# Loading the input and the first two weight blocks in four feature parts, with both projections run part by part

## The chip, the cores and the metric

The kernel runs on one core of a Trainium2 chip. The metric is the device time of one execution in microseconds, the median of several. Before the change it is 2222.32 us (three runs, 2222.03 to 2223.93).

## What is computed

The reference is a stack of three blocks on one sequence of 512 tokens with 1024 features, all in 32-bit floats. Only the very beginning matters here:

```
h = rms_norm(x, norm_g[layer])      # x: 512 x 1024
p = h @ w_in[layer]
c_q, c_kv, k_r, gate_a, dil_qkv, gate_b = split(p)
```

`dil_qkv` holds queries, keys and values of three groups of dilated attention; the queries and keys are rotated by tables of sine and cosine. After two layers of this come a feed-forward block, a mix of a recurrence and windowed attention, and a second feed-forward block.

## The kernel before

It is written by hand, engine by engine, with a semaphore for each kind of event; every engine executes its instructions strictly in the order of its own program.

**Layout.** The input is kept transposed: X holds eight tiles (k = 0 to 7) of 128 features by 512 tokens. The input rows are loaded into XIN (part of ARENA) by SyncE and turned by TensorE in 32 transposes of 128x128 (lines 1082 to 1091), eight for each pair of tiles, which VectorE copies from PSUM to X (line 2038).

**Three-part products.** Each operand of a large product is split in a high part (ScalarE, rounded to fp32r) and a low part (VectorE, the rest). A product is then three matmuls, high by high, low by high and high by low (`three`, lines 870 to 872). For X they are UH (`hi_of_gained`, line 1309, which also applies the gain of the norm) and UL (`lo_of_gained`, line 1767). For the weights they are WH (`hi_of_chunk`, line 1290) and WL (`lo_of_chunk`, line 1716).

**Weight chunks.** Weights come in chunks of 1024 rows by 256 columns (1 MB), numbered in order of use: chunk 0 is the first query projection q0, chunk 1 the key projection k0, chunk 2 the value projection v0, chunk 3 q1, chunk 4 k1. WS, WH and WL each have two slots, for even and odd chunks. SyncE loads chunk c into WS when chunk c-2 has been split completely (`load`, line 773, semaphore w_split). ScalarE makes the high part of chunk c when the product with chunk c-2 is finished. A `feature_major` product (q and k) is eight steps k of six matmuls of 512 columns, a `token_major` one (v) 96 matmuls of 256 columns.

**The norm.** The inverse root mean square of each token is applied after the products. ScalarE squares the tiles of X (line 1299), VectorE adds them up in RB (lines 1729 and 1732), TensorE sums over partitions (`norm_sum`, line 920) and, after VectorE has taken the reciprocal, turns it back (`norm_spread`, line 936); ScalarE copies it to RI (line 1322). With RI, VectorE scales the rotation tables (lines 2096 and 2097) and then rotates q0 and k0 (`rotated`, lines 1806 to 1817).

**The order at the start.** TensorE: one small transpose of the gains, 32 transposes of the input, q0, the transposes of all gain vectors and one small product for a bias table (lines 1124 and 1128), k0 with the norm's parts between its steps, v0, q1, k1. VectorE takes the results of lines 1124 and 1128 in `vectors` and `bias_rows` (lines 2043 to 2056), and computes eight small values in `softplus` (lines 2063 to 2077), between which it waits for an exponential from ScalarE (line 1523). GpSimd's queue loads the rotation tables (line 814) and the masks (line 815), ScalarE's queue the small vectors.

## Time and profile before

| what | value |
|---|---|
| median of three runs | 2222.32 us |
| lowest and highest run | 2222.03 and 2223.93 us |
| the profiled execution's own time | 2223.23 us |
| its span | 2221.4 us |
| TensorE busy (matmul) | 96% of the span |
| VectorE, ScalarE, GpSimd busy | 52%, 35%, 2% |
| DMA, mean over the span | 85 GB/s |

The span is the time from the first to the last recorded instruction of the profiled execution; its own time is 1.8 us longer. TensorE is busy nearly all the time, so what counts is where it waits, and at which clock it runs. The chain of work that ended last lies on TensorE for 87% of the span, on VectorE for 8%. All that the change touches lies in the first 80 us.

### The profile page before, as it was taken

What the parts mean: (1) busy time and instruction counts of PE and PEld (TensorE: products, weight loads), DVE (VectorE), ACT (ScalarE), POOL (GpSimd) and SP (SyncE); (2) the same over time, 40 slices, a digit from 0 to 9 for tenths busy, and PEclk for the clock granted to TensorE, in tenths of its full rate; (3) what the DMA queues carried; (4) which work ended last, traced back from release to release, by engine and by line L of the source; (5) the groups of instructions that cost most, each with busy time, mean ns of one, the idle gap of its engine ahead of it and who ended that gap; (6) DMA issues with size and microseconds to landing.
All of it is one profiled execution on the core that took longest, in us unless ns stands there. A gap on an engine that the chain in (4) does not pass through costs nothing.

```text
span 2221.4 us, 28281 instructions
## 1 busy us (share of the span) xinstructions
PE 2130.4 (96%) x11693; PEld 1756.8 (79%) x11693; DVE 1160.5 (52%) x1593; ACT 775.7 (35%) x1229; POOL 40.0 (2%) x75
## 2 busy tenths in 40 slices
PE   6999999999999999989999998999999989999997
PEld 5888878678888887767888887787688877888886
DVE  5655557645565556746333335775653446333334
ACT  3251434633241535524222224353632234222223
POOL 0101000000001000000000000000000000000000
PEclk9999999999999999999999999999999999999998
DMA  5423222013313122123233321234023221333221
GB/s 161 114 58 95 77 76 77 22 58 109 100 39 114 58 69 67 39 86 114 94 95 103 103 98 57 76 114 133 21 87 102 96 94 58 95 95 108 99 95 38
DMA packets 157280, 188.49 MB, mean 85 GB/s; under 512 B 4018, under 2 KB 147700, under 8 KB 157044
## 3 DMA queue, kind: packets, MB, share of 16 engines
q1 hardware_dynamic: 152256, 174.34, 24.9%
q0 software_dynamic: 4464, 12.47, 1.8%
q8 instruction: 79, 1.29, 0.2%
q14 instruction: 29, 0.24, 0.0%
q10 hardware_dynamic: 452, 0.15, 0.0%
HBM read 181.68 MB, written 7.36 MB: 85 GB/s over the span
## 4 chain that ended last, share of the span: by engine, by line
PE 87%; DVE 8%; ACT 3%; issue 2%; DMA 1%; SPq 0%; DVEq 0%; ACTq 0%
PE PS L870 26%; PE PS L872 25%; PE PS L871 25%; PE PS L956 4%; PE PS L997 2%; PE PS L968 2%; DVE WL L1716 1%; PE PS L1075 1%; DVE TMP L1966 1%; DVE UL L1767 1%; ACT PR L1362 1%; DMA ARENA<-in_x 1%; ACT PR L1359 0%; DVE PS L1822 0%; DVE X L1974 0%
## 5 line engine op out<-in xcount | busy, mean ns | idle before, releaser
L870 PE MATMUL PS<-UH,WH 128*128 128x512 f32 x1712 | 677.1, 396 | 28.5 <-DVE UL L1767 17.5
L872 PE MATMUL PS<-UH,WL 128*128 128x512 f32 x1712 | 670.5, 392 | 0.0
L871 PE MATMUL PS<-UL,WH 128*128 128x512 f32 x1712 | 670.1, 391 | 0.0
L1290 ACT ACTIVATE WH<-WS 128x2048 fp32r<-128x2048 f32 x103 | 197.3, 1916 | 630.0 <-PE PS L872 630.0
L870 PEld LDWEIGHTS PS<-UH,WH 128*128 128x128 f32 x1712 | 324.2, 189 | 102.5 <-issue 26.5
L872 PEld LDWEIGHTS PS<-UH,WL 128*128 128x128 f32 x1712 | 323.6, 189 | 68.7
L871 PEld LDWEIGHTS PS<-UL,WH 128*128 128x128 f32 x1712 | 324.3, 189 | 66.9 <-issue 0.7
L1716 DVE TENSOR_TENSOR WL<-WS,WH 128x2048 fp32r<-128x2048 f32 x103 | 235.8, 2289 | 238.2 <-ACT WH L1290 238.0
L1987 DVE TENSOR_TENSOR WL<-WS,WH 128x2048 fp32r<-128x2048 f32 x44 | 100.7, 2289 | 157.9 <-ACT WH L1445 157.9
L1445 ACT ACTIVATE WH<-WS 128x2048 fp32r<-128x2048 f32 x44 | 84.3, 1917 | 264.5 <-PE PS L872 264.5
L870 PE MATMUL PS<-HH,WH 128*128 128x512 f32 x352 | 136.9, 389 | 0.0
L871 PE MATMUL PS<-HL,WH 128*128 128x512 f32 x352 | 136.9, 389 | 0.0
L872 PE MATMUL PS<-HH,WL 128*128 128x512 f32 x352 | 136.9, 389 | 0.0
L870 PE MATMUL PS<-WH,UH 128*128 128x256 f32 x416 | 118.5, 285 | 0.0
L871 PE MATMUL PS<-WL,UH 128*128 128x256 f32 x416 | 117.7, 283 | 0.0
L872 PE MATMUL PS<-WH,UL 128*128 128x256 f32 x416 | 117.7, 283 | 0.0
L968 PE MATMUL PS<-IDN,PR 128*128 128x128 f32 x624 | 89.3, 280 | 17.6 <-DVE PT L1851 7.5
L968 PEld LDWEIGHTS PS<-IDN,PR 128*128 128x128 f32 x624 | 66.4, 140 | 42.7 <-issue 28.9
L997 PE MATMUL PS<-PT,ARENA 128*64 128x128 f32 x1248 | 84.7, 279 | 1.3 <-DVE ARENA L1876 1.3
L2004 DVE TENSOR_TENSOR ARENA<-PS,RI 128x1024 f32 (+1 forms) x22 | 26.9, 1224 | 112.3 <-PE PS L872 112.3
L870 PEld LDWEIGHTS PS<-WH,UH 128*128 128x128 f32 x416 | 79.7, 192 | 1.0 <-issue 0.2
L871 PEld LDWEIGHTS PS<-WL,UH 128*128 128x128 f32 x416 | 79.7, 192 | 0.6 <-issue 0.2
(270 smaller groups left out, 2713.2 us busy)
## 6 DMA issues: line engine op xcount, KB each, us to landing
WS<-in_ffn_w SPq DMA_DIRECT2D x66, 1024.0 KB, 5.2
WS<-in_w_in SPq DMA_DIRECT2D x64, 1024.0 KB, 5.4
WS<-in_w_out SPq DMA_DIRECT2D x8, 1024.0 KB, 5.2
WS<-in_w_gate SPq DMA_DIRECT2D x8, 1024.0 KB, 5.4
WS<-in_w_attn_out SPq DMA_DIRECT2D x4, 1024.0 KB, 5.1
WS<-in_w_lru_out SPq DMA_DIRECT2D x4, 1024.0 KB, 5.2
WS<-in_w_o SPq DMA_DIRECT2D x4, 1024.0 KB, 5.1
bias_skewed<-bias_rows POOLq DMA_DIRECT2D x1, 3072.0 KB, 14.7
```

Of the source, the lines that this page charges most:

```text
L870: nc.tensor.matmul(dst, sh, mh, start=start, stop=False, skip_group_check=True)
L871: nc.tensor.matmul(dst, sh, ml, start=False, stop=False, skip_group_check=True)
L872: return nc.tensor.matmul(dst, sl, mh, start=False, stop=stop, skip_group_check=True)
L956: last[b] = nc.tensor.matmul(acc[:, c0:c0 + w], q, k, start=start, stop=True, skip_group_check=True)
L968: last = nc.tensor.transpose(bank(4 + b)[:, k * P:(k + 1) * P], PR[:, n % 2, b * S + k * P:b * S + (k + 1) * P], IDN[:, :])
L997: last = nc.tensor.matmul(dst, v, PT[:, n % 2, k * P:(k + 1) * P], start=start, stop=stop, skip_group_check=True)
L1075: last = nc.tensor.matmul(pair(key)[:, w, :], RGW[:, w, 2 * j + m, :], XC[:, m, :], start=True, stop=True)
L1290: nc.scalar.activation(WH[:, c % 2, 0:kt * n], WS[:, c % 2, 0:kt * n], ACT.Copy).then_inc(w_hi, 1)
L1445: nc.scalar.activation(WH[:, c % 2, :], WS[:, c % 2, :], ACT.Copy).then_inc(w_hi, 1)
L1716: tt(WL[:, c % 2, 0:kt * n], WS[:, c % 2, 0:kt * n], WH[:, c % 2, 0:kt * n].bitcast(F32), ALU.subtract).then_inc(w_split, 1)
L1987: tt(WL[:, c % 2, :], WS[:, c % 2, :], WH[:, c % 2, :].bitcast(F32), ALU.subtract).then_inc(w_split, 1)
L2004: tt(hid, pair((f, "w3", 0)), ri, ALU.mult).then_inc(dve_out, 1)
```

## The change

The input is loaded in four parts of 256 features (all tokens), each followed by the same 256 rows of chunk 0 and of chunk 1; each part has its own semaphores. Rotation tables and masks are issued only when the last input part has landed. TensorE turns one input part, multiplies what it can of q0 and k0, turns the next, and so on (`input_turned`, `first_step`); ScalarE and VectorE split input and weights by the same parts. q0 and k0 are thus worked on together, the norm's two TensorE parts move into v0, the small transposes and the bias product move between the steps of k0, and their results are taken by VectorE before it copies the last input part. The high and low parts of chunks 2 and 3 are both made before VectorE takes the reciprocal of the norm. The PSUM banks change where that is needed.

```diff
--- before.py
+++ after.py
@@ -489,7 +489,10 @@
-        x_in = sem("x_in")
+        x_in = [sem(f"x_in{f}") for f in range(4)]
+        first_in = [sem(f"first_in{f}") for f in range(4)]
+        first_hi = sem("first_hi")
+        first_lo = sem("first_lo")
...
@@ -606,6 +609,13 @@
+        def landing(c):
+
+            return 16 * (c // 2)
+
+        def first_part(t, c, f):
+            return slot(t, c, KD, CW)[:, 2 * f:2 * f + 2, :]
+
@@ -763,13 +773,17 @@
-            for r in range(NT):
-                sp.dma_start(XIN[:, r, :], a["x"][0].rearrange("(i r) d -> r i d", r=NT)[r]).then_inc(x_in, 16)
+            for f in range(4):
+                feats = slice(f * CW, (f + 1) * CW)
+                sp.dma_start(XIN[:, :, feats], a["x"][0][:, feats].rearrange("(i r) d -> i r d", r=NT)
+                             ).then_inc(x_in[f], 16)
+                for c in range(2):
+                    sp.dma_start(slot(WS, c, KD, CW)[:, 2 * f:2 * f + 2, :],
+                                 chunk_source(pl.chunks[c][0])[:, 2 * f:2 * f + 2, :]).then_inc(first_in[f], 16)
 
             def load(c, src):
                 key, kt, n, _ = pl.chunks[c]
-                if c >= 2:
-                    sp.wait_ge(w_split, c - 1)
+                sp.wait_ge(w_split, c - 1)
                 sp.dma_start(slot(WS, c, kt, n), src).then_inc(landed[c % 2], 16)
...
-            c = 0
+            c = 2
@@ -811,6 +825,7 @@
             pool.dma_start(SK[:, :], bass.AP(a["attn_sinks_2"].tensor, 0, [[0, P], [1, QH]])).then_inc(rel_in, 16)
+            pool.wait_ge(x_in[3], 16)
             pool.dma_start(TAB, a["rotation"]).then_inc(tabs_in, 16)
             pool.dma_start(MASK[:, :, :], a["dil_mask"]).then_inc(tabs_in, 16)
             pool.wait_ge(small_dve, 3)
@@ -897,13 +912,17 @@
-            def token_major(key):
+            def token_major(key, norm=None):
 
                 c = pl.chunk[key]
                 take_pair(key)
                 weights(c)
                 acc = pair(key).rearrange("p a (b n) -> p (a b) n", b=2)
                 for k in range(KD):
+                    if norm and k == 2:
+                        norm_sum(norm, KD)
+                    if norm and k == 4:
+                        norm_spread(norm)
                     for t in range(NT):
                         tok = slice(t * P, (t + 1) * P)
 
@@ -1078,17 +1097,71 @@
 
             pe.wait_ge(identity_in, 16)
             pe.wait_ge(gains_in, 16)
-            nc.tensor.transpose(bank(5)[:, 0:FIRST], ROWS[0:FIRST, 0, :], IDN[0:FIRST, 0:FIRST]).then_inc(small_pe, 1)
-            pe.wait_ge(x_in, 16 * NT)
-            for j in range(4):
-                key = ("xt", j)
-                take_pair(key)
+            nc.tensor.transpose(bank(7)[:, 0:FIRST], ROWS[0:FIRST, 0, :], IDN[0:FIRST, 0:FIRST]).then_inc(small_pe, 1)
+
+            def input_turned(f):
+
+                key = ("xt", f)
+                pe.wait_ge(x_in[f], 16)
+                if f == 1:
+                    pe.wait_ge(small_dve, 1)
+                if f >= 2:
+                    pe.wait_ge(dve_out, pl.dve_out["xt", f - 2])
                 for m in range(2):
                     for r in range(NT):
                         last = nc.tensor.transpose(pair(key)[:, m, r * P:(r + 1) * P],
-                                                   XIN[:, r, (2 * j + m) * P:(2 * j + m + 1) * P], IDN[:, :])
+                                                   XIN[:, r, (2 * f + m) * P:(2 * f + m + 1) * P], IDN[:, :])
                 last.then_inc(acc_ready, 1)
+
+            def first_step(c, k):
+
+                key = pl.chunks[c][0]
+                pe.wait_ge(lo_done, pl.lo[("x", 0), k])
+                if k < 6:
+                    pe.wait_ge(first_lo, k // 2 * 2 + c + 1)
+                else:
+                    weights(c)
+                for m in range(2):
+                    part = slice(m * P, (m + 1) * P)
+                    last = three(pair(key)[:, m, :], slot(WH, c, KD, CW)[:, k, part], slot(WL, c, KD, CW)[:, k, part],
+                                 UH[:, k, :], UL[:, k, :], k == 0, k == KD - 1)
+                if k == KD - 1:
+                    last.then_inc(acc_ready, 1)
+
+            def vectors_turned():
+                pe.wait_ge(dve_out, pl.dve_out["xt", 2])
+                pe.wait_ge(consts_in, 16 * vector_dmas)
+                for i in range(2):
+                    n = min(P, NVEC - i * P)
+                    last = nc.tensor.transpose(bank(5)[:, i * P:i * P + n], ROWS[0:n, i, :], IDN[0:n, 0:n])
+                last.then_inc(small_pe, 1)
+
+                pe.wait_ge(rel_in, 48)
+                nc.tensor.matmul(bank(4)[0:QH, 0:384], TBL, ONEHOT, start=True, stop=True).then_inc(small_pe, 1)
+
+            input_turned(0)
+            first_step(0, 0)
+            input_turned(1)
+            first_step(0, 1)
+            first_step(0, 2)
+            input_turned(2)
+            first_step(0, 3)
+            first_step(1, 0)
+            first_step(1, 1)
+            first_step(0, 4)
+            input_turned(3)
+            first_step(0, 5)
+            first_step(1, 2)
+            first_step(1, 3)
+            vectors_turned()
+            first_step(1, 4)
+            first_step(1, 5)
+            first_step(0, 6)
+            first_step(0, 7)
+            first_step(1, 6)
+            first_step(1, 7)
             pe.wait_ge(const_ok, 2)
+
...
@@ -1106,27 +1179,19 @@
             for L in range(DEPTH):
                 for hh in range(2):
                     for i, (w, g) in enumerate(DILATED_ORDER):
+                        if L == 0 and hh == 0 and i < 2:
+                            continue
                         if w == "v":
                             if hh == 0 and g == 0:
                                 if L == 0:
                                     pe.wait_ge(small_dve, 3)
+                                    pe.wait_ge(dve_out, pl.dve_out["xt", 3])
                                 else:
                                     results_taken(pl.item_at["mla", L - 1][1])
-                            token_major((w, L, hh, g))
+                            token_major((w, L, hh, g), ("x", 0) if (L, hh, g) == (0, 0, 0) else None)
                         else:
                             feature_major((w, L, hh, g), new=("x", L) if hh == 0 and i == 0 else None,
                                           norm=("x", L) if hh == 0 and i == 1 else None)
-                        if L == 0 and hh == 0 and i == 0:
-
-                            pe.wait_ge(consts_in, 16 * vector_dmas)
-                            for i in range(2):
-                                n = min(P, NVEC - i * P)
-                                last = nc.tensor.transpose(bank(5 + i)[:, 0:n], ROWS[0:n, i, :], IDN[0:n, 0:n])
-                            last.then_inc(small_pe, 1)
-
-                            pe.wait_ge(rel_in, 48)
-                            nc.tensor.matmul(bank(7)[0:QH, 0:384], TBL, ONEHOT, start=True, stop=True
-                                             ).then_inc(small_pe, 1)
                     pe.wait_ge(rope_done, pl.rope["k", L, hh, 2])
                     attention(("dil", L, hh), lambda: token_major(("v", L, hh, 2)))
                 for j in range(2):
@@ -1496,15 +1560,21 @@
             for L in range(DEPTH):
                 if L == 0:
                     act.wait_ge(small_dve, 1)
-                    for k in range(KD):
-                        hi_of_gained(("x", L), k, (dve_out, pl.dve_out["xt", k // 2]))
-                        if k == 3:
-                            hi_of_chunk(0)
-                    hi_of_chunk(1)
+                    for f in range(4):
+                        for k in (2 * f, 2 * f + 1):
+                            hi_of_gained(("x", L), k, (dve_out, pl.dve_out["xt", f]))
+                        act.wait_ge(first_in[f], 32)
+                        for c in range(2):
+                            nc.scalar.activation(first_part(WH, c, f), first_part(WS, c, f), ACT.Copy
+                                                 ).then_inc(first_hi if f < 3 else w_hi, 1)
+                        squares(("x", L), lambda k: X[:, k, :], (2 * f, 2 * f + 1))
+                else:
+                    squares(("x", L), lambda k: X[:, k, :], range(KD))
+                table(ACT.Sqrt)
                 c0 = pl.chunk["q", L, 0, 0]
-                squares(("x", L), lambda k: X[:, k, :], range(KD))
-                table(ACT.Sqrt)
                 hi_of_chunk(c0 + 2)
+                if L == 0:
+                    hi_of_chunk(c0 + 3)
                 rms(("x", L), D)
                 copy_inverse(("x", L))
 
@@ -1516,7 +1586,7 @@
-                        if hh == 1 or i > 0:
+                        if hh == 1 or i > (L == 0):
                             hi_of_chunk(pl.chunk[key] + 2)
                         if L == 0 and hh == 0 and i == 2:
                             act.wait_ge(small_dve, 4)
@@ -2031,17 +2101,13 @@
             dve.wait_ge(small_pe, 1)
-            nc.vector.tensor_copy(G[:, 0:FIRST], bank(5)[:, 0:FIRST]).then_inc(small_dve, 1)
-            for j in range(4):
-                key = ("xt", j)
-                ready(key)
-                nc.vector.tensor_copy(X[:, 2 * j:2 * j + 2, :], pair(key)).then_inc(dve_out, 1)
+            nc.vector.tensor_copy(G[:, 0:FIRST], bank(7)[:, 0:FIRST]).then_inc(small_dve, 1)
 
...
@@ -2079,17 +2145,31 @@
                 if L == 0:
-                    for k in range(KD):
-                        lo_of_gained(("x", L), k)
-                        if k == 3:
-                            lo_of_chunk(0)
-                    lo_of_chunk(1)
-                add_squares(("x", L), 0, KD)
+                    for f in range(4):
+                        key = ("xt", f)
+                        ready(key)
+                        nc.vector.tensor_copy(X[:, 2 * f:2 * f + 2, :], pair(key)).then_inc(dve_out, 1)
+                        for k in (2 * f, 2 * f + 1):
+                            lo_of_gained(("x", L), k)
+                        for c in range(2):
+                            if f < 3:
+                                dve.wait_ge(first_hi, 2 * f + c + 1)
+                            else:
+                                dve.wait_ge(w_hi, c + 1)
+                            tt(first_part(WL, c, f), first_part(WS, c, f), first_part(WH, c, f).bitcast(F32),
+                               ALU.subtract).then_inc(first_lo if f < 3 else w_split, 1)
+                        add_squares(("x", L), 2 * f, 2 * f + 2)
+                        if f == 2:
+                            vectors()
+                            bias_rows()
+                else:
+                    add_squares(("x", L), 0, KD)
                 if L == 0:
-                    vectors()
-                    bias_rows()
+                    lo_of_chunk(c0 + 2)
+                    lo_of_chunk(c0 + 3)
                 inverse(("x", L))
-                lo_of_chunk(c0 + 2)
+                if L:
+                    lo_of_chunk(c0 + 2)
                 if L == 0:
                     dve.wait_ge(tabs_in, 32)
                 dve.wait_ge(inv_copied, pl.copied["x", L])
@@ -2100,7 +2180,7 @@
                         key = (w, L, hh, g)
                         if w != "v":
                             rotated(key)
-                        if hh == 1 or i > 0:
+                        if hh == 1 or i > (L == 0):
                             lo_of_chunk(pl.chunk[key] + 2)
                         if L == 0 and hh == 0 and i == 1:
                             softplus()
```

The order of instructions on VectorE, from the start. Before (L2038 copies to X, L1767 makes UL, L1716 makes WL, L1732 adds squares, L2043 takes the vectors):

```order
L2038 COPY X<-PS 128x1024 [waits acc_ready] x4
L1767 SCALAR_TENSOR_TENSOR UL<-X,G,UH 128x512 [waits hi_done] x4
L1716 TENSOR_TENSOR WL<-WS,WH 128x2048 [waits w_hi]
L1767 SCALAR_TENSOR_TENSOR UL<-X,G,UH 128x512 [waits hi_done] x4
L1716 TENSOR_TENSOR WL<-WS,WH 128x2048 [waits w_hi]
L1729 COPY RB<-SQ 128x512 [waits sq_ready]
L1732 TENSOR_TENSOR RB<-RB,SQ 128x512 [waits sq_added,sq_ready] x7
L2043 COPY G<-PS 128x112 [waits small_pe]
```

In the change, its third and fourth part (L2151 copies to X, L1837 makes UL, L2159 makes WL, L1802 adds squares, L2109 takes the vectors, L2119 the bias table; L1786 are the low parts of chunks 2 and 3):

```order
L2151 COPY X<-PS 128x1024 [waits acc_ready]
L1837 SCALAR_TENSOR_TENSOR UL<-X,G,UH 128x512 [waits hi_done] x2
L2159 TENSOR_TENSOR WL<-WS,WH 128x512 [waits first_hi] x2
L1802 TENSOR_TENSOR RB<-RB,SQ 128x512 [waits sq_added,sq_ready] x2
L2109 COPY G<-PS 128x112 [waits small_pe]
L2110 COPY G<-PS 128x34
...
L2119 TENSOR_SCALAR PT<-PS 16x384 [waits small_pe]
L2122 TENSOR_SCALAR NSK<-SK 128x16 [waits rel_in]
L2151 COPY X<-PS 128x1024 [waits acc_ready,dve_step]
L1837 SCALAR_TENSOR_TENSOR UL<-X,G,UH 128x512 [waits hi_done] x2
L2159 TENSOR_TENSOR WL<-WS,WH 128x512 [waits w_hi] x2
L1802 TENSOR_TENSOR RB<-RB,SQ 128x512 [waits sq_added,sq_ready] x2
L1786 TENSOR_TENSOR WL<-WS,WH 128x2048 [waits w_hi] x2
L1808 RECIPROCAL RC<-RC 128x4 [waits std_ready]
```

The four copies to X, which stood together, now stand apart, and the wait for the vectors' transposes (small_pe) stands ahead of the fourth; the low parts of chunks 2 and 3 now both stand ahead of the reciprocal.

The order on TensorE around the vectors' transposes. Before, between the last step of q0 and the first of k0:

```order
L872 MATMUL PS<-UH,WL 128x512
L1124 MATMUL PS<-IDN,PR 128x128 [waits consts_in]
L1124 MATMUL PS<-IDN,PR 128x34
L1128 MATMUL PS<-PT 16x384 [waits rel_in]
L870 MATMUL PS<-UH,WH 128x512 [waits w_split,dve_out]
```

In the change, between steps 3 and 4 of k0:

```order
L887 MATMUL PS<-UH,WL 128x512
L1136 MATMUL PS<-IDN,PR 128x128 [waits consts_in,dve_out]
L1136 MATMUL PS<-IDN,PR 128x34
L1140 MATMUL PS<-PT 16x384 [waits rel_in]
L885 MATMUL PS<-UH,WH 128x512 [waits first_lo,lo_done]
```

They stood behind 48 matmuls of q0. Now they stand behind ten steps (steps 0 to 5 of q0, 0 to 3 of k0, 60 matmuls) and all 32 transposes of the input, and ahead of the last six steps.

## Rows read from the trace of the kernel before

**Rows 1.** The page's first part: busy time, share of the span, instructions.
```profile
PE 2130.4 (96%) x11693; PEld 1756.8 (79%) x11693; DVE 1160.5 (52%) x1593; ACT 775.7 (35%) x1229; POOL 40.0 (2%) x75
```
**Rows 2.** Busy time by stage; the last three columns are granted clock, DMA share, GB/s.
```profile
0.00:13.30 13.30, 0.26 (x1) 0.18 (x1) 0.17 (x1) 0.00 (x0) 3.23 (x11) 1.00 0.87 289
13.30:16.60 3.30, 3.27 (x16) 3.04 (x16) 1.22 (x1) 0.00 (x0) 0.00 (x0) 1.00 1.10 348
...
19.00:22.90 3.90, 0.00 (x1) 0.00 (x0) 3.86 (x6) 3.90 (x6) 0.00 (x0) 1.00 0.03 11
22.90:25.30 2.40, 0.00 (x0) 0.00 (x0) 2.40 (x3) 2.40 (x5) 0.00 (x0) 0.50 0.00 0
25.30:29.70 4.40, 4.33 (x10) 3.47 (x11) 4.40 (x5) 2.31 (x3) 0.00 (x0) 0.50 0.79 235
...
51.90:63.60 11.70, 11.70 (x97) 11.47 (x95) 11.47 (x14) 1.92 (x1) 0.00 (x0) 1.00 0.28 89
63.60:64.90 1.30, 0.00 (x1) 0.00 (x0) 1.30 (x2) 1.26 (x4) 0.00 (x0) 1.00 0.00 0
```
**Rows 3.** TensorE in order of time: start, duration, engine, line, [idle before <-releaser].
```profile
13.32 3.04 PEld L1088 LDWEIGHTS PS<-IDN,ARENA 128*128 128x128 f32 x16 [7.56 <-DMA ARENA<-in_x]
16.61 0.85 PEld L1088 LDWEIGHTS PS<-IDN,ARENA 128*128 128x128 f32 x8 [0.25 <-DVE X L2038]
...
25.37 0.77 PE L870 MATMUL PS<-UH,WH 128*128 128x512 f32 x1 [6.37 <-DVE WL L1716]
...
38.39 0.45 PE L1124 MATMUL PS<-IDN,PR 128*128 128x128 f32 x2
...
39.51 0.50 PE L870 MATMUL PS<-UH,WH 128*128 128x512 f32 x1
...
50.10 0.60 PE L936 MATMUL PS<-IDN,RB 128*128 128x128 f32 x4
...
64.97 0.47 PE L870 MATMUL PS<-UH,WH 128*128 128x512 f32 x1 [1.37 <-DVE WL L1716]
75.98 0.39 PE L870 MATMUL PS<-UH,WH 128*128 128x512 f32 x1
```
**Rows 4.** VectorE in order of time.
```profile
15.33 4.94 DVE L2038 COPY X<-PS 128x1024 f32<-128x1024 f32 x4 [9.25 <-PE PS L1088]
20.18 2.73 DVE L1767 SCALAR_TENSOR_TENSOR UL<-X,G,UH 128x512 fp32r<-128x512 f32 x4
22.83 2.28 DVE L1716 TENSOR_TENSOR WL<-WS,WH 128x2048 fp32r<-128x2048 f32 x1
...
38.88 0.28 DVE L2043 COPY G<-PS 128x112 f32<-128x112 f32 x1 [2.99 <-PE PS L1124]
...
40.09 0.15 DVE L2056 TENSOR_SCALAR NSK<-SK 128x16 f32<-128x16 f32 x1
...
51.43 0.69 DVE L2096 TENSOR_TENSOR ARENA<-ARENA,RI 128x512 f32<-128x512 f32 x1 [0.82 <-ACT RI L1322]
...
62.54 2.29 DVE L1716 TENSOR_TENSOR WL<-WS,WH 128x2048 fp32r<-128x2048 f32 x1
...
68.57 0.17 DVE L2067 TENSOR_SCALAR SP__84<-SP__84 128x8 f32<-128x8 f32 x1 [3.67 <-ACT SP__84 L1523]
...
72.04 2.29 DVE L1716 TENSOR_TENSOR WL<-WS,WH 128x2048 fp32r<-128x2048 f32 x1
```
**Rows 5.** ScalarE in order of time.
```profile
16.66 1.28 ACT L1309 ACT_TABLE_LOAD   x1 [16.66 <-DVE X L2038]
17.95 2.56 ACT L1309 ACTIVATE UH<-X,G 128x512 fp32r<-128x512 f32 x4
...
50.73 0.60 ACT L1322 ACTIVATE RI<-PS 128x512 f32<-128x512 f32 x1 [3.06 <-PE PS L936]
```
**Rows 6.** Groups by line and shape: busy, mean ns of one, idle before.
```profile
L1290 ACT ACTIVATE WH<-WS 128x2048 fp32r<-128x2048 f32 x103 | 197.3, 1916 | 630.0 <-PE PS L872 630.0
L1380 ACT ACTIVATE WH<-WS 128x512 fp32r<-128x512 f32 x36 | 22.8, 633 | 0.0
L1930 DVE TENSOR_TENSOR WL<-WS,WH 128x512 fp32r<-128x512 f32 x36 | 24.7, 686 | 14.5 <-ACT WH L1380 14.5
```
**Rows 7.** DMA: landing of the four input loads (L767); weight loads up to 60 us.
```profile
DMA to landing us min/median/max: 4.2/6.3/11.1
WS<-in_w_in SPq DMA_DIRECT2D x5, 1024.0 KB, 5.5
```

More of the change, by code:

```diff
@@ L1376, in hi_part @@
                 if i == 0:
-                    act.wait_ge(landed[c % 2], 16 * (c // 2 + 1))
+                    act.wait_ge(landed[c % 2], landing(c))
                     act.wait_ge(acc_ready, pl.acc[pl.chunks[c - 2][3]])
@@ L1442, in hi_in_loop @@
                     c = c0 + b
-                    act.wait_ge(landed[c % 2], 16 * i + 16 * ((c + 2) // 2 + 1))
+                    act.wait_ge(landed[c % 2], 16 * i + landing(c + 2))
                     act.wait_ge(acc_ready, 2 * i + (pl.acc[f, "w1", 0] + b))
```

11 lines of the change are left out of this document (5 added, 6 removed).

## Prediction

> **What bounds the kernel now.** I read the page's shares first. TensorE is busy for 2130.4 us of a span of 2221.4 [rows 1], so a change can take from the 91 us in which it stands still, or from its slow clock. The change touches only the start, so the second view is the stages of the first 65 us. TensorE does nearly nothing in the first 13.3 us, while the DMA engines are busy for 87% of the time at 289 GB/s [rows 2]. Then it turns the input, stands still from 19.0 to 25.3 and runs ten matmuls at a granted clock of 0.50 (the 1.2 GHz level), the rest at 1.00 (2.4 GHz). The third view, TensorE in order of time, has the points that I measure against [rows 3]: q0 starts at 25.37 after a wait of 6.37 us for the low weights, k0 at 39.51; after 1.37 us of another wait q1 starts at 64.97, and k1 follows at 75.98 without one. The stage of v0 begins at 51.9 and has 96 matmuls in 11.5 us, 0.12 us each [rows 2]. A later start of k1 is a later end, since nothing waits there but TensorE.
>
> The pace of a 512-column matmul: at the low clock 4.4 us for ten, 0.43 each [rows 2]; q0 takes 13.02 us from 25.37 to 38.39 [rows 3], so its other 38 take 8.6 us, 0.227 each. A step of six costs 1.36 us or, slow, 2.6. Eight transposes cost 1.5 us at the beginning (16 in 3.04) and 0.85 later [rows 3].
>
> **The change, along its path.** (1) *First part.* The first input load landed 4.2 us after its issue [rows 7], at 5.0; it was as large as a new input part. In the change eight transposes, right behind the gains' one (ended at 5.9), give their result at 7.7. Then: copy to X 1.24 (4.94 for four [rows 4]), table load 1.28, two high parts of X at 0.62 (2.56 for four, the last with its latency [rows 5]), a quarter of high weights 0.63, a quarter of low weights 0.69 [rows 6], and about 0.3 for semaphores. The first step of q0 starts at 13.3, not 25.37. I take it at the slow pace: before, the first sixteen transposes too ran at 0.19 us each and the next eight at 0.106 [rows 3], though the clock column shows 1.00 for both. All parts land in time: each is 1.05 MB, at 289 to 348 GB/s [rows 2] 3.0 to 3.6 us, so the last is there by about 17.5 while its weights are needed at 40. That the weights' 1 KB runs went at 348 GB/s [rows 2] is the reason why I charge nothing for the input's new 1 KB runs. **12.1 us are gained here, for the moment.**
>
> (2) *The engines take turns.* TensorE's program has the second part's transposes behind that first step: 2.7 us slow plus 0.85 to 1.5, result at 17.1. From there to the low weights is again copy, two high parts, quarter and quarter: 4.3 us. TensorE has one step (1.4) to fill that, so it stands for 3 us, until 21.5. It then does (q0,2) and the third transposes (to 24.7), and three steps (to 29.7), by which time the third part is split. Then follow (q0,4), the fourth transposes, (q0,5), (k0,2) and (k0,3), four steps and 0.85 us, to 35.9.
>
> (3) *VectorE is held.* It has finished its third part at 30.9, and the next in its order is the copy of the vectors, which waits for transposes that stand behind (k0,3) on TensorE. Result at 36.3. Vectors and bias took 1.36 us (38.88 to 40.24 [rows 4]); the copy of the last input part, queued behind them, starts at 37.6 though its transposes ended at 32. Chain as in (2): the last quarter of low weights of q0 is ready at 41.8. TensorE had two steps left, to 39.6, and stands for 2.3 us. Six behind: the last four steps take 5.5 us, to 47.5, or to 49.3 with a slow stretch.
>
> (4) *Chunk 2.* Its load waits for that same quarter. Loads of a chunk took 5.5 us in the median [rows 7], high and low part 1.92 and 2.29 [rows 6, 4]; with semaphores v0 starts at 41.8 + 5.5 + 1.9 + 2.3 + 0.3 = 51.8. Before, it was 51.9, the load being hidden behind q0. **All of the 12.1 us is given back.** TensorE waits another 2.5 us here.
>
> (5) *q1.* v0 now contains the norm's small products, which took about 0.9 us in k0: 12.3 us, to 64.1. The wait before q1 goes (1.37 us), since chunk 3 is split early: q1 starts 0.8 us sooner than 64.97.
>
> (6) *k1.* The norm is now spread in the middle of v0, behind four of its eight steps: 51.8 + 5.7 + 0.5 (the sums) puts the four transposes at 58.0, and with their 0.60 [rows 3], ScalarE's 0.60 [rows 5] and semaphores RI comes at 59.4. Before, VectorE's chain from the scaled tables at 51.43 to the end of chunk 4's low part (72.04 + 2.29) took 22.9 us [rows 4]. Without chunk 3's low part (2.2) and without most of the wait for the exponential (3.67, of which 0.3 stays; its table load now runs ahead) it takes 17.3: 76.8. k1 starts at 77.0, not 75.98: **+1.0 us**, with a wait of 1.9 us, where there was none.
>
> (7) *The clock.* After 3.9 us without work the granted clock had fallen to the 1.2 GHz level, and after 4.4 us of work it was back [rows 2]; that stretch cost ten times 0.2, 2.0 us. Now TensorE stands five times for 2 to 6 us instead of once for 6.3. One slow step is in (1) already. None more is the lower bound (0), three more the upper (6 us). I take one that isn't covered by a wait: +2.0, since the waits are shorter than the one in the row, which lets the clock survive some.
>
> Sum: -0.1 (v0's start: -12.1 from (1), +12.0 from (2) to (4)), +0.8 (the norm's parts in v0), -1.4 (the wait before q1), +1.9 (the wait before k1), which is +1.0 by the two starts of k1 (the terms are rounded), and +2.0 for the clock: **+3.0 us**. Against the profiled execution (2223.23) that is 2226.2; this one lies 0.9 above the median of 2222.32, so I predict 2225.3. About 0.2%, 4.4 us, is what a measurement of this kernel can tell from no change; the forecast is within it. Moved at no cost: tables and masks (issued at about 15, ready by 26 even with the 11.1 us of the slowest input load [rows 7], used at 59.5), the squares (ScalarE and VectorE both have gaps in (2)), chunk 4's load (issued at 51.6, used at 66).
>
> **Rivals.** *TensorE gets to the vectors in time (faster).* If VectorE weren't held in (3), the last copy would start at 31.9 instead of 37.6, and v0, q1 and k1 would all be 5.7 us sooner: 1.0 - 5.7 = -4.7, 2217.6. It decides itself at 30.9: TensorE must have done ten steps and four transposes by then, 60 matmuls at 0.227 and 3.4 us, 17.0 us from 13.3 on. For it speaks that 30.3 is just possible; against it that the first step is slow and the 3 us wait of (2) is on the way. Chance 0.08, all of it beyond 0.2% faster.
>
> *The clock stays down (slower).* Where work comes in pieces of one to three steps, each wait may bring the low level back, and a piece of 4 us may pass before it goes. It decides when three or more slow stretches of 2.0 us lie outside a wait: +1.0 + 3 x 2.0 = +7.0, 2229.3; with every one of the 96 matmuls slow it would be 19 us, less the 8 us of waits that they would fill, +12. For it speaks the fall in [rows 2] and that TensorE, ahead of VectorE in (2) and (3), can't work them off; against it the stage of q1, where a wait of 1.3 us [rows 2] left the clock at 1.00. The Trainium skill, "TensorE: Matmul & The Clock Gate", section "HAM oscillation — how this bites in real kernels", speaks for this rival: short bursts with waits for data between them lose the fast clock each time, and it advises to run all k tiles in one go before waiting. By that rule the sum is the +7.0 above; by the 1.3 us wait in the row alone it is +1.0. Chance 0.26.
>
> *The parts don't come one by one (the change does nothing new).* The twelve loads are in flight together and could finish together, at about 17.5. The first step would then start near 24, 11 us later than in (1), but with no waits in (2): the ten steps, transposes and vectors of (2) and (3) take 18.1 us at the fast pace, so that the vectors come near 42 instead of 36.3, and all behind them 5.7 us later: +8.7. Against it: four input loads in flight landed 4.2 to 11.1 us after their issue [rows 7], one after the other. I count it in the slower rival's chance, with 0.03 of it.
>
> **How the numbers follow.** Forecast 0.66, faster rival 0.08, slower rival 0.26. The forecast's case goes from -1 (no slow stretch, a fast load of chunk 2) to +4.4. The range goes on to both sides of it until some 0.06 is left out below (the faster rival's far end) and 0.10 above (the slower one beyond +8.7): 2219.5 to 2231.0. Faster by over 0.2%: 0.08, within 0.2%: 0.66, slower by over 0.2%: 0.26.
>
> **What would show it.** Right: first 512-column matmul near 13.3; VectorE's idle time before the copy of the vectors (5 us), released by TensorE; the last copy to X near 37.6; v0 at 51 to 53, released by chunk 2's low part; an idle time of 1 to 3 us before k1, released by chunk 4's low part. Wrong: v0 before 48 (then (3) or (4) isn't on the path), or the landing of an input part that releases TensorE after the first; and a granted clock below 1.00 for more than 12 us of the first 90.

## The result, and the profile after

The change takes 2229.75 us (median of ten runs, 2225.1 to 2231.48) against 2223.51 for the kernel before (ten runs on the same chip): a ratio of 1.0026, with a 95% interval of 1.0017 to 1.0035. Run again beside the experiments it was at 1.0021 (1.0012 to 1.0030). The difference of the medians is +6.2 us in the first comparison and +4.6 in the second; +3.0 (2225.3 us) was forecast. The profiled execution of the change took 2230.66 us with a span of 2228.7, 7.3 longer than the span before.

The page's first part, to be held against [rows 1]: TensorE is busy 4.7 us longer, though it has the same number of matmuls.

```profile
PE 2135.1 (96%) x11693; PEld 1760.5 (79%) x11693; DVE 1161.3 (52%) x1599; ACT 775.6 (35%) x1235; POOL 39.9 (2%) x75
```

TensorE in order of time (start, duration, engine, line, [idle before <-releaser]), to be held against [rows 3]:

```profile
5.25 1.97 PE L1112 MATMUL PS<-IDN,ARENA 128*128 128x128 f32 x8 [0.35 <-DMA ARENA<-in_x]
14.74 0.76 PE L885 MATMUL PS<-UH,WH 128*128 128x512 f32 x1 [7.52 <-DVE WL L2159]
...
23.56 0.77 PE L885 MATMUL PS<-UH,WH 128*128 128x512 f32 x1 [2.39 <-DVE WL L2159]
...
26.26 1.39 PE L1112 MATMUL PS<-IDN,ARENA 128*128 128x128 f32 x8
...
33.33 1.04 PE L1112 MATMUL PS<-IDN,ARENA 128*128 128x128 f32 x8
...
38.31 0.45 PE L1136 MATMUL PS<-IDN,PR 128*128 128x128 f32 x2
...
44.38 0.47 PE L885 MATMUL PS<-UH,WH 128*128 128x512 f32 x1 [1.96 <-DVE WL L2159]
...
55.17 0.55 PE L885 MATMUL PS<-WH,UH 128*128 128x256 f32 x1 [5.10 <-DVE WL L1786]
...
70.71 0.40 PE L885 MATMUL PS<-UH,WH 128*128 128x512 f32 x1
...
83.33 0.47 PE L885 MATMUL PS<-UH,WH 128*128 128x512 f32 x1 [1.55 <-DVE WL L1786]
```

q0 starts 10.6 us sooner than before (14.74 against 25.37), but v0 (55.17 against the 51.9 of [rows 2]) is 3.3 late, q1 5.7 late (70.71 against 64.97) and k1 7.35 late (83.33 against 75.98). The span grew by 7.3 us, so for this pair of executions nothing is gained or lost behind k1. So the loss has three pieces: 3.3 us up to v0, 2.5 more inside v0, and the wait before k1.

VectorE and ScalarE, the rows that answer to [rows 4, 5]:

```profile
7.26 1.22 DVE L2151 COPY X<-PS 128x1024 f32<-128x1024 f32 x1 [2.14 <-PE PS L1112]
...
32.24 1.48 DVE L1802 TENSOR_TENSOR RB<-RB,SQ 128x512 f32<-128x512 f32 x2
38.80 0.27 DVE L2109 COPY G<-PS 128x112 f32<-128x112 f32 x1 [5.08 <-PE PS L1136]
...
40.20 1.23 DVE L2151 COPY X<-PS 128x1024 f32<-128x1024 f32 x1
...
43.55 1.29 DVE L2159 TENSOR_TENSOR WL<-WS,WH 128x512 fp32r<-128x512 f32 x2
...
52.73 2.29 DVE L1786 TENSOR_TENSOR WL<-WS,WH 128x2048 fp32r<-128x2048 f32 x1 [6.50 <-ACT WH L1354]
...
65.86 0.69 DVE L2176 TENSOR_TENSOR ARENA<-ARENA,RI 128x512 f32<-128x512 f32 x1 [3.18 <-ACT RI L1386]
...
80.90 2.29 DVE L1786 TENSOR_TENSOR WL<-WS,WH 128x2048 fp32r<-128x2048 f32 x1
```

```profile
5.67 1.52 ACTq L1553 DMA_DIRECT2D PR<-in_rg_a_b  x1
...
10.10 0.32 ACTq L1553 DMA_DIRECT2D PR<-in_ffn_post_g  x1
10.53 1.28 ACT L1373 ACT_TABLE_LOAD   x1 [10.53 <-issue]
...
50.79 1.91 ACT L1354 ACTIVATE WH<-WS 128x2048 fp32r<-128x2048 f32 x1 [4.40 <-DMA WS<-in_w_in]
```

VectorE stands 5.08 us ahead of the vectors while the last input part, whose transposes began at 33.33 and lasted 1.04, waits behind them. ScalarE's table load starts at 10.53, although the first copy to X was over at 8.48 (7.26 + 1.22). It stood behind the queue's own DMA issues, which last to 10.42.

Stages by windows (columns as in [rows 2]: after the four engines and GpSimd come granted clock, DMA share, GB/s):

```profile
23.56:26.97 3.41, 3.41 (x10) 2.73 (x11) 1.75 (x3) 0.50 (x1) 0.00 (x0) 0.50 0.00 0
54.28:61.11 6.83, 5.94 (x28) 5.97 (x29) 3.04 (x2) 1.24 (x1) 0.00 (x0) 0.50 0.76 232
61.11:70.47 9.36, 9.36 (x79) 9.36 (x80) 5.18 (x8) 0.86 (x2) 0.00 (x0) 1.00 0.18 56
```

A granted clock of 0.50 is the 1.2 GHz level. Twice TensorE works at it with no wait to cover the loss: from 23.56 to 26.97, and for the beginning of v0 (to 61.11).

### The profile page after: what moved, and what is told of

Its sections match the earlier page's. It is cut to its first block, busy times and chain, and to the rows that moved or that the text cites. A ratio compares the mean times of both kernels' runs of the same rounds, so it can differ in the third digit from the quotient of the medians.

```text
span 2228.7 us, 28317 instructions
## 1 busy us (share of the span) xinstructions
PE 2135.1 (96%) x11693; PEld 1760.5 (79%) x11693; DVE 1161.3 (52%) x1599; ACT 775.6 (35%) x1235; POOL 39.9 (2%) x75
## 4 chain that ended last, share of the span: by engine, by line
PE 86%; DVE 8%; ACT 3%; issue 2%; ACTq 0%; DMA 0%; DVEq 0%
PE PS L885 25%; PE PS L887 25%; PE PS L886 25%; PE PS L975 4%; PE PS L1016 2%; PE PS L987 2%; DVE WL L1786 1%; PE PS L1094 1%; DVE UL L1837 1%; DVE TMP L2036 1%; ACT PR L1426 1%; ACT PR L1423 0%; DVE PS L1892 0%; DVE X L2044 0%; ACTq L1553 0%
## 5 line engine op out<-in xcount | busy, mean ns | idle before, releaser
L887 PE MATMUL PS<-UH,WL 128*128 128x512 f32 x1712 | 671.0, 392 | 0.0
L887 PEld LDWEIGHTS PS<-UH,WL 128*128 128x128 f32 x1712 | 324.2, 189 | 68.3
L1786 DVE TENSOR_TENSOR WL<-WS,WH 128x2048 fp32r<-128x2048 f32 x101 | 231.3, 2290 | 245.2 <-ACT WH L1354 245.1
L2057 DVE TENSOR_TENSOR WL<-WS,WH 128x2048 fp32r<-128x2048 f32 x44 | 100.7, 2289 | 157.9 <-ACT WH L1509 157.9
L887 PE MATMUL PS<-HH,WL 128*128 128x512 f32 x352 | 137.0, 389 | 0.0
L887 PE MATMUL PS<-WH,UL 128*128 128x256 f32 x416 | 118.8, 285 | 0.0
```

What stands on the lines that cost most here:

```text
L887: return nc.tensor.matmul(dst, sl, mh, start=False, stop=stop, skip_group_check=True)
L1786: tt(WL[:, c % 2, 0:kt * n], WS[:, c % 2, 0:kt * n], WH[:, c % 2, 0:kt * n].bitcast(F32), ALU.subtract).then_inc(w_split, 1)
L2057: tt(WL[:, c % 2, :], WS[:, c % 2, :], WH[:, c % 2, :].bitcast(F32), ALU.subtract).then_inc(w_split, 1)
```

## The experiments

All differences and ratios are to executions of the kernel before, run beside each group of experiments; their medians are 2223.51 us (beside the change), 2224.10 (a0_again to e3), 2224.93 (e4, e5, b1, e6) and 2223.91 (e7, e8, e9, t1). Most rows have ten or eleven executions, e6 six and e7 eight. A twelfth of e1 took 5249.98 us, which nothing here explains, and is left out. The last four columns are of the one profiled execution: its own time, the first matmuls of v0 and k1 (the 49th matmul from the start of q1), and "low", how much of its first 90 us it spent at a granted clock of 0.50.

| run | median us | to before | ratio (95%) | profiled us | v0 | k1 | low us |
|---|---|---|---|---|---|---|---|
| before | 2223.51 | | | 2223.23 | 51.92 | 75.98 | 6.8 |
| the change | 2229.75 | +6.2 | 1.0026 (1.0017 to 1.0035) | 2230.66 | 55.17 | 83.33 | 10.2 |
| a0_again | 2228.71 | +4.6 | 1.0021 (1.0012 to 1.0030) | 2226.59 | 54.04 | 80.83 | 3.4 |
| e1_vectors_behind | 2222.90 | -1.2 | 0.9997 (0.9988 to 1.0006) | 2221.95 | 47.70 | 74.75 | 3.4 |
| e2_vectors_by_sync | 2228.32 | +4.2 | 1.0017 (1.0008 to 1.0026) | 2227.15 | 51.36 | 79.31 | 6.8 |
| e3_chunk2_in_parts | 2226.74 | +2.6 | 1.0011 (1.0002 to 1.0019) | 2227.35 | 53.01 | 79.98 | 6.8 |
| e4_clock_held | 2227.54 | +2.6 | 1.0010 (1.0001 to 1.0019) | 2227.88 | 55.76 | 81.25 | 6.8 |
| e5_softplus_later | 2226.25 | +1.3 | 1.0011 (1.0002 to 1.0020) | 2231.25 | 56.21 | 81.52 | 13.6 |
| b1_tables_last_alone | 2222.22 | -2.7 | 0.9986 (0.9977 to 0.9995) | 2222.22 | 51.07 | 75.12 | 6.8 |
| e6_all_mended | 2217.77 | -7.2 | 0.9972 (0.9960 to 0.9984) | 2218.53 | 47.78 | 73.11 | 6.8 |
| e8_vectors_and_softplus | 2221.99 | -1.9 | 0.9994 (0.9985 to 1.0003) | 2219.39 | 48.34 | 72.14 | 0 |
| e9_and_by_sync | 2218.69 | -5.2 | 0.9977 (0.9967 to 0.9986) | 2218.57 | 47.68 | 73.01 | 6.8 |
| e7_mended_and_clock_held | 2216.95 | -7.0 | 0.9971 (0.9961 to 0.9982) | 2216.61 | 45.65 | 69.47 | 0 |
| t1_tables_not_last | 2229.74 | +5.8 | 1.0023 (1.0014 to 1.0032) | 2228.50 | 53.02 | 81.20 | 6.8 |

A profiled execution is one of the ten or so, and what lies behind k1 varies too: its own time less k1 is 2147.3 us before and in the change, and between 2145.4 and 2149.7 in the others. So v0 and k1 are read for what moved in the program, and the medians for what it is worth.

### The change once more

> The change as it stands, once more, beside the others on one chip. First result: +6.2 us against before (2229.75 to 2223.51). All theories: +5 to +7.5 us; the other runs of this call are read against this one.

+4.6 us, a little below the 5 to 7.5 expected. Its profiled execution is the fastest of its eleven. It began q0 1.1 us later than the first one (at 15.84, since ScalarE's DMA issues lasted to 11.52) and still reached v0 1.1 and k1 2.5 us sooner. Stages by windows of this execution:

```profile
44.30:49.00 4.70, 4.70 (x22) 3.70 (x20) 0.92 (x2) 1.17 (x2) 0.00 (x0) 1.00 1.01 300
49.00:54.00 5.00, 0.16 (x1) 0.00 (x0) 2.29 (x1) 3.43 (x2) 0.00 (x0) 0.96 0.44 140
54.00:57.05 3.05, 3.01 (x14) 3.04 (x15) 2.29 (x1) 0.39 (x1) 0.00 (x0) 0.51 0.65 184
57.05:68.20 11.15, 11.15 (x96) 11.15 (x96) 5.37 (x8) 0.86 (x2) 0.00 (x0) 1.00 0.42 139
```

Same kernel, same wait before v0 (4.88 us), but v0 is slow until 57.05 instead of 61.11, and there was no slow stretch near 24. So two executions of one kernel differ in how long ScalarE's issues last, which moved q0, and in the clock, which moved v0 and k1.

### VectorE freed from the vectors

```diff
-                        if f == 2:
+                        if f == 3:
                             vectors()
                             bias_rows()
```

> The change, with the vectors and the bias taken by VectorE behind its fourth part, not behind its third. Theory (VectorE is held by a wait for work that stands late on TensorE): the copy of the fourth part starts when its transposes end, at about 34.4 and not 40.2; the wait before step 6 of q0 (1.96 us) goes, v0 starts 5.6 us sooner; 5 to 7 us faster than the change. Rival 1 (TensorE is the bound there anyway): at most the 1.96 us wait goes, 2 us faster. Rival 2 (the slow clock is the loss, the waits only move): within 1 us of the change.

5.8 us less in the median than a0_again (some 5.3 by the ratios); v0 6.3 us sooner than there. VectorE and ScalarE in order of time:

```profile
32.40 1.23 DVE L2151 COPY X<-PS 128x1024 f32<-128x1024 f32 x1 [0.68 <-PE PS L1112]
...
45.26 2.29 DVE L1786 TENSOR_TENSOR WL<-WS,WH 128x2048 fp32r<-128x2048 f32 x1 [5.74 <-ACT WH L1354]
```

```profile
43.24 1.92 ACT L1354 ACTIVATE WH<-WS 128x2048 fp32r<-128x2048 f32 x1 [4.65 <-PE PS L887]
```

The last copy starts as soon as its transposes are done (32.40 for 40.20), and the high part of chunk 2 is no longer released by the DMA but by TensorE, which has finished q0 (L887). So the step of the prediction holds: one wait in VectorE's order carried on through the slot, the load and v0. Taken away, it gives back the whole 4.6 us: the kernel is level with the one before (0.9997). The wait before k1 is still there (1.56 us).

### ScalarE's table load freed from its DMA issues

Sixteen small loads are moved from ScalarE's queue to SyncE's, behind the twelve loads of the parts:

```diff
-                    nc.scalar.dma_start(ROWS[r:r + m, at_row // P, :], src[done:done + m, :]
-                                        ).then_inc(consts_in if at_row else gains_in, 16)
+                    if not at_row:
+                        nc.scalar.dma_start(ROWS[r:r + m, 0, :], src[done:done + m, :]).then_inc(gains_in, 16)
...
+                    if at_row:
+                        sp.dma_start(ROWS[r:r + m, at_row // P, :], src[done:done + m, :]).then_inc(consts_in, 16)
```

> The change, with the sixteen small vector loads issued by SyncE behind its twelve loads, so that ScalarE issues two loads only. Theory (ScalarE's own issues, which lasted until 10.42, held the table load that could start at 8.5, and all that follows hangs on it one after the other): first 512-column matmul at about 12.8 and not 14.74, all of it passed on: 1.9 us faster than the change. Rival (a later wait absorbs it, since TensorE and VectorE both have gaps): first matmul sooner but v0 at the same time, within 0.5 us of the change.

ScalarE in order of time:

```profile
8.74 1.28 ACT L1388 ACT_TABLE_LOAD   x1 [8.74 <-DVE X L2166]
```

The cause of the late first step is shown: the table load is now released by the copy and q0 starts at 12.95, where in a0_again the load starts at 11.63 and q0 at 15.84. The gain is not: the medians differ by 0.4 us, and within the intervals there may be none. v0 came 2.7 us sooner and k1 1.5, since v0 ran slow for longer (it took 15.3 us for 14.2). The expected saving of about 2 us was missed.

### Chunk 2 in four parts

Each quarter of chunk 2 is loaded as soon as the quarter of its slot is split:

```diff
...
-            c = 2
+            for f in range(4):
+                if f < 3:
+                    sp.wait_ge(first_lo, 2 * f + 1)
+                else:
+                    sp.wait_ge(w_split, 1)
+                sp.dma_start(slot(WS, 2, KD, CW)[:, 2 * f:2 * f + 2, :],
+                             chunk_source(pl.chunks[2][0])[:, 2 * f:2 * f + 2, :]).then_inc(early_in, 16)
+            c = 3
...
```

> The change, with chunk 2 loaded in four parts, each as soon as the low weights of the same part of chunk 0 are made, so that only 256 KB are left to load behind the last one. Theory (the load of chunk 2, 6.5 us behind the last quarter of chunk 0, is what v0 waits for): high part of chunk 2 at about 47.5 and not 50.8, v0 3.3 us sooner, still waiting some 1.8 us; 3 to 5 us faster than the change (the upper end if the slow clock behind v0's start goes too). Rival (the splitting of chunk 2 is held by q0 or by VectorE): less than 1 us faster.

2.0 us less than a0_again, where 3 to 5 were expected and less than 1 by the rival; the intervals of the two ratios overlap. The high part of chunk 2 starts at 48.62 for the 47.5 expected. ScalarE:

```profile
48.62 1.91 ACT L1365 ACTIVATE WH<-WS 128x2048 fp32r<-128x2048 f32 x1 [2.29 <-DMA WS<-in_w_in]
```

It still waits for a landing: the last quarter can't be issued before VectorE has split the last quarter of chunk 0. It was issued at 44.20 and took 4.4 us to ScalarE's start, where the whole chunk of 1 MB took 6.5. The load is on the path as predicted, but a quarter of the size took two thirds of the time. Whether the rest is a fixed time of a load or comes from the load of chunk 3, issued 0.6 us behind, isn't shown.

### The clock held before v0

```diff
             pe.wait_ge(const_ok, 2)
+            pe.wait_ge(small_dve, 2)
+            for _ in range(18):
+                nc.tensor.matmul(bank(5), UH[:, 0, 0:P], UH[:, 7, :], start=True, stop=True, skip_group_check=True)
```

> The change, with eighteen matmuls of 512 columns whose result nobody reads between the last step of k0 and v0, where TensorE waits for some 5 us. Theory (the clock falls in that wait, and the beginning of v0 runs at 1.2 GHz): v0 starts when it did, since the eighteen take 4.1 us of the 5, but at the full clock; granted clock 1.00 from there on; 1.5 to 3.5 us faster than the change (which was 2228.7 in the last call). Rival (the slow stretch only fills a wait for VectorE that comes anyway, before k1): less than 1 us, and a longer wait before k1.

Stages by windows:

```profile
44.92:48.33 3.41, 3.41 (x10) 2.64 (x9) 1.38 (x3) 1.61 (x3) 0.00 (x0) 0.50 0.83 226
...
55.70:68.60 12.90, 12.90 (x110) 12.86 (x110) 7.66 (x9) 0.86 (x2) 0.00 (x0) 1.00 0.52 164
```

v0 runs at 1.00 from its start and takes 12.8 us (55.76 to 68.60), 2.7 less than the 15.5 of the change (55.17 to 70.71). That is the price of its slow beginning. k1 came as much sooner behind v0 (25.5 us for 28.2), so the slow stretch was not hidden in the wait before k1, as the rival had it. This execution fell to 0.50 at 44.92 instead, behind the wait of 1.96 us. The filler matmuls so began late, at 51.68, and held v0 for 0.6 us: the low part of chunk 2 was ready at 55.12. In the medians 2.0 us remain against a0_again and 3.6 against the first comparison, within intervals that overlap.

### Softplus behind the low part of chunk 4

```diff
-                        if L == 0 and hh == 0 and i == 1:
+                        if L == 0 and hh == 0 and i == 2:
                             softplus()
```

> The change, with the softplus values computed on VectorE behind the low part of chunk 4, not ahead of it. Theory (VectorE's chain behind the norm, which now ends in the middle of v0, is late for k1): the wait before k1, 1.55 us, is gone and 1.6 us are gained on the change. Rival (k1 has to wait for the rotation of k0 or for the high part anyway): less than 0.5 us.

+1.3 to before, where the change has +4.6 and +6.2. The row of VectorE, ahead of the softplus now:

```profile
76.86 2.29 DVE L1786 TENSOR_TENSOR WL<-WS,WH 128x2048 fp32r<-128x2048 f32 x1
```

The low part ends at 79.15 (76.86 + 2.29), 2.4 us before k1 starts, and the trace has no wait there. The step is right. The saving in the medians (3.3 us on a0_again) is larger than the 1.55 us of that wait; by the ratios (1.0011, some +2.4 us, for 1.0021) it is 2.2, and the intervals overlap. The profiled execution is the slowest of its eleven, 5.0 us above the median. Up to q1 its program on TensorE, VectorE and ScalarE is that of the change, so it shows what the change can meet too: 13.6 us at the low clock and v0 at 56.21.

### Tables last, alone and taken away

```diff
             pool.dma_start(SK[:, :], bass.AP(a["attn_sinks_2"].tensor, 0, [[0, P], [1, QH]])).then_inc(rel_in, 16)
+            pool.wait_ge(x_in, 16 * NT)
             pool.dma_start(TAB, a["rotation"]).then_inc(tabs_in, 16)
```

This is the edit in the kernel before (b1); in t1 the corresponding wait is taken out of the change.

> The kernel before with one part of the change alone: GpSimd's queue issues the rotation tables and the masks when the input has landed. Theory (the 1.3 MB of tables share the DMA engines with the input): the input lands at 9 to 10 and not at 13.3, q0 starts 3 to 4 us sooner, and all behind it, with no new wait: 3 to 4 us faster than before. Rival (chunk 0 or the small vectors' loads hold q0, or the tables come too late for the rotations): within 1 us of before.

> The change without GpSimd's wait ahead of the rotation tables: they are in flight with the input parts and first weights from the start. In the kernel before the wait alone was worth 2.7 us. Theory: here parts 1 to 3 have to spare (only the first part's landing is on the path), so only the first part matters: if it lands 1 us later the first matmul comes at 15.5 to 16 instead of 14.7, and the time is up to 1 us above the change's, no more. Rival: the later parts land late enough to release TensorE; then 3 us or more are lost and the trace shows waits for in_x or in_w_in after 10 us.

TensorE in b1, to be held against [rows 3]:

```profile
11.91 4.51 PE L1089 MATMUL PS<-IDN,ARENA 128*128 128x128 f32 x24 [5.50 <-DMA ARENA<-in_x]
...
24.33 0.77 PE L871 MATMUL PS<-UH,WH 128*128 128x512 f32 x1 [6.37 <-DVE WL L1717]
```

In the kernel before, that one line is worth 1.4 us on the input's transposes (11.91 for the 9 to 10 expected), 1.0 on q0, 0.9 at k1 and, between the two profiled executions, 1.0 in the whole (2222.22 for 2223.23). In the medians it is 2.7, below the 3 to 4 expected: the kernel before had a median of 2224.93 here, 1.7 above its profiled execution. The interval of the ratio reaches from 1.1 to 5.1 us, so the 1.0 of the traces is just below it. In the change it is worth nothing that can be measured (1.0023 without, 1.0021 and 1.0026 with): the first part is there near 5.0 either way, and no later part releases TensorE, although the slowest input part landed 13.9 us after its issue instead of 8.6. The part of the change that helps alone is made idle by the rest.

### The mended versions

e8 has the edits of e1 and e5; e9 also that of e2; e6 also that of e3; e7 is e6 with the filler of e4, six matmuls instead of eighteen (`range(6)`).

> The change with all four edits: vectors taken behind the fourth part, small vectors issued by SyncE, chunk 2 loaded in four parts, softplus behind the low part of chunk 4. Theory: the gains of the first (5.3 us), of the earlier table load (1.9) and of the softplus (1.6) add up; the parts of chunk 2 give nothing more, since its high part then waits for q0 itself: v0 at about 46, k1 at about 70, 8 to 9 us faster than the change, 4 us faster than before. Rival (each removed wait shows the next one, and the clock falls in them): no more than 6 us faster than the change, as before or 1 us better.

> The change with two moves: the vectors are taken behind the fourth part on VectorE (as in e1_vectors_behind) and the softplus stands behind chunk 4's low part (as in e5_softplus_later). If the two savings are independent, 5.3 us from the first and the wait of 1.5 us before k1 from the second add up: about 7 us below the change, 2.0 us below the kernel before (ratio 0.999). If the version with all four moves (3 per mille faster than before) owes its gain to the earlier loads, this one stays within 1 us of e1_vectors_behind (ratio 0.9997). v0 near 47.7, k1 near 73.2.

> As e8_vectors_and_softplus, and the small vectors issued by SyncE (as in e2_vectors_by_sync), so that ScalarE's table load isn't held up. First 512-column matmul near 12.9 instead of 15, v0 1 to 2 us earlier than in e8. Theory: the time saved at the very start reaches k1 now that nothing else holds VectorE: ratio about 1 us below e8's. Rival: as in e2 alone, TensorE's clock gives it back (same as e8 within 0.5 us); then the four-move version owes its rest to chunk 2 in parts.

> The version with all four moves (e6_all_mended), and six extra 512-column matmuls into an unused bank ahead of v0, which nobody reads (work added, no part of the computation). They fill the wait of 1.8 us before v0. If that wait is what makes v0's start slow (49.3 to 52.7 at the 1.2 GHz level in e6), this gains 1 to 2 us over e6 (ratio 0.9965); if the clock falls because of how thin the work was long before, nothing is gained and the six matmuls may cost up to 1 us (ratio 0.9975).

**e6, e7 and e9 beat both kernels**: 0.9972, 0.9971 and 0.9977, some 5 to 7 us below the kernel before, where 4 had been expected of e6. e8 is at 0.9994, and its interval holds 1; its -1.9 us are the 2.0 expected. So e2's edit, worth next to nothing in the change, is worth 3.3 us here (e9 against e8), more than the 1 us expected, while chunk 2 in parts adds nothing that the intervals separate. The traces don't show where the 3.3 us are: e8's profiled execution is the fastest of its eleven, 2.6 us below their median and without any slow stretch in the first 90 us, while e9's lies at its median. It reached k1 0.9 us sooner than e9's, although it began q0 2.3 us later (15.00 against 12.71). TensorE of the two, third transposes:

```profile
25.25 1.04 PE L1112 MATMUL PS<-IDN,ARENA 128*128 128x128 f32 x8
```

```profile
23.97 1.66 PE L1127 MATMUL PS<-IDN,ARENA 128*128 128x128 f32 x8
```

From a lead of 2.3 us at q0 e9 has 1.3 left here; it worked at the low clock from 21.83 to 25.24. The filler of e7 shortened the wait before v0 from 1.83 to 0.47 and its execution had no slow stretch in the first 90 us, but the ratio is that of e6, between the 0.9965 and 0.9975 expected for the two cases, and e8's execution had no slow stretch without a filler: whether six matmuls hold the clock is undecided.

## Why the prediction was right, and what was mis-sized

The range held the time and the path was the one described; the size, +3.0, was too small. The forecast's own case ended at +4.4, below both +4.6 and +6.2. The range held them because it had been carried on for the slower case, which had a chance of 0.26 from 0.2% on; the ratio of 1.0026 lies there, though its interval begins at 1.0017. So the path was foreseen, and the size was held partly by luck. The third rival, that the parts don't come one by one, is ruled out: the first was there when its transposes began at 5.25.

**(1) First part: gain right, 1.4 us too large.** 14.74 against 13.3. The parts landed in time, and only the first landing releases TensorE. The sum let the table load follow the copy. It forgot the order of ScalarE's own queue: eighteen DMA issues, over at 8.49 before (the last is 7.41 + 1.08), now last to 10.42 and hold the table load 2.0 us. e2 shows it by taking sixteen of them away.

**(2) Turns: order right, sum wrong.** Waits of 2.39 for 3.0, 1.96 for 2.3. From 21.5 to 29.7 the sum has 8.2 us for four steps and eight transposes, which by its own prices are 6.3 (4 x 1.36 and 0.85); no term stands for the other 1.9. TensorE took 8.3 us for this part (23.56 to 31.87), of which 1.7 were a slow stretch. So the sum came out there by an error that happened to be as long as a stretch that (7) didn't foresee. Everything is 2.1 us late at 23.56, 1.4 of it from (1) and most of the rest from the second transposes at the slow pace, and still 2.4 late at the vectors (38.31 for 35.9). By its own prices the sum would have come to about +1.1.

**(3) VectorE held: right**, and shown by e1. Idle 5.08 us where "5 us" stood; last copy at 40.20 for 37.6, which is the delay of (1) and (2). The rival that TensorE reaches the vectors by then did not occur, but e1 brings about what it would have given: 5.3 to 5.8 us for the 5.7 that it was priced at.

**(4) Chunk 2: right, 0.9 us too short.** The load was issued at 44.27 and released ScalarE at 50.79, 6.5 us for the 5.5 taken from [rows 7]. v0 at 55.17 for 51.8: 2.5 of it late start, 0.9 load. The wait before v0 is 5.10 us for 2.5.

**(5) v0: 0.6 us too short** at the full clock (12.8 to 12.9 in e4, e7 and e8 for 12.3); the wait before q1 is gone, as said.

**(6) k1: right.** VectorE's chain from RI to the end of chunk 4's low part is 17.3 us (65.86 to 83.19), to the tenth what the sum had. The wait is 1.55 for 1.9; e5 removes it.

**(7) Clock: this is the term that failed in size.** One uncovered stretch, +2.0, was taken, because the waits were shorter than the one seen before, "which lets the clock survive some". In the change's profile there were two, the second twice as long as the first: about 2.7 us at v0, and near 24 some 1.7 (six matmuls in 2.7 us, 23.56 to 26.26, instead of 1.36, and 0.35 more for eight transposes), which are part of the delay in (2). All executions together give the price at v0: it takes 12.8 to 12.9 us without a slow stretch (e4, e7, e8), 14.2 to 14.4 with 3.0 to 3.4 us of it (a0_again, e1, e3, e5, e6, e9) and 15.3 to 15.6 with 5.5 to 6 (the change, e2, t1).

The granted clock was below 1.00 for 10.2 us of the first 90, under the 12 that would have told the other case; in e5's execution, with the same program up to q1, it was 13.6. The rival "the clock stays down" named this mechanism, and its price of three stretches, +7.0, is nearer the first comparison (+6.2) than the forecast is. The Trainium skill, "TensorE: Matmul & The Clock Gate", section "HAM oscillation — how this bites in real kernels", says that bursts with data waits between them lose the fast clock again and again; the trace agrees for v0's start (slow after each of its waits of 4.9 to 5.4 us, in the change, a0_again, e2 and t1) but not for each wait, as the last section shows.

## What to carry to other kernels

When work is cut into pieces so that it can begin sooner, follow each in-order engine past the piece: here the first product began 10.6 us sooner and everything was lost at one small copy that stood ahead of a large one, then at a slot, then at the load behind it. Look also at what an engine's queue issues before its first computation. Where medians differ by a few us, compare several executions: k1 of one and the same kernel came at 83.33 us in one and at 80.83 in another.

## What was not expected of the hardware

**DMA issues take longer while other loads are on the way.** ScalarE's issue of the same small load (rg_a_b) took 0.32 us before and 1.52 in the change, beside twelve issues of SyncE instead of six. SyncE in order of time, before (three lines), then in the change, then in e2, where ScalarE issues nothing after 1.6 us:

```profile
0.75 2.02 SPq L767 DMA_DIRECT2D ARENA<-in_x  x4
2.81 4.29 SPq L773 DMA_DIRECT2D WS<-in_w_in  x2
...
50.64 0.37 SPq L773 DMA_DIRECT2D WS<-in_w_in  x1
```

```profile
9.08 2.12 SPq L781 DMA_DIRECT2D WS<-in_w_in  x2
```

```profile
9.46 2.04 SPq L781 DMA_DIRECT2D WS<-in_w_in  x2
```

A chunk of 1 MB issued alone took 0.37 us, two of them right behind the input loads 4.29. In the change the first two quarters took 1.11 us and the last two 2.12, with or without ScalarE's issues beside them (2.04 in e2). So the size of a load doesn't set the length of its issue, SyncE's last issues aren't slowed by ScalarE's, and in both kernels the long ones come a few us behind the first loads. What holds them stays open.

**A longer wait doesn't make the clock fall.** Before the third step of q0 the twelve executions with input parts fall into two groups. Waits of 2.08 to 2.73 us were followed by a granted clock of 0.50 (the change 2.39, e3 2.55, e4 2.08, e5 2.73, e6 2.24, e9 2.26), waits of 2.81 to 2.84 by 1.00 (a0_again, e1, e2, e7, e8, t1): it fell behind the shorter ones. In the first group TensorE was still slow in the step ahead of the wait (its first matmul took 0.68 to 0.78 us, in the second group 0.47 to 0.56), so the step ended later and the wait was shorter. What makes the clock fall there isn't shown. Before v0, 1.83 us in e6 were followed by 0.50, some 1.5 us behind the start of v0, and 1.83 in e8 by 1.00; waits of 4.88 to 5.42 us there were followed by 0.50 each time (four executions). TensorE of e6 and e8 at v0:

```profile
47.78 0.36 PE L908 MATMUL PS<-WH,UH 128*128 128x256 f32 x1 [1.83 <-DVE WL L1812]
```

```profile
48.34 0.36 PE L885 MATMUL PS<-WH,UH 128*128 128x256 f32 x1 [1.83 <-DVE WL L1786]
```
